# A transformer block and two hybrid attention and retention layers: V of the attention heads projected in one product of 512 columns, V stationary in the retention heads

## The reference

```python
def hybrid_layer(x, norm_gain, w_in, w_out, rel_bias, cos, sin):
    hn = rms_norm_2(x, norm_gain)
    proj = hn @ w_in                       # 1024 -> 4096
    aq, ak, av, ag, rq, rk, rv, rg = jnp.split(proj, cuts, axis=-1)    # 512 each
    ya = chunked_rel_attention(aq, ak, av, rel_bias)      # 8 heads of 64
    yr = chunkwise_retention(rq, rk, rv, cos, sin)        # 4 heads of 128, rms_norm_2 per head
    y = jnp.concatenate([ya * silu(ag), yr * silu(rg)], axis=-1)
    return x + y @ w_out
```

## Time and profile before

| | us |
|---|---|
| median of three runs | 1198.65 |
| the three runs | 1197.14, 1198.65, 1198.66 |
| the profiled execution | 1195.86 |
| span of its trace | 1193.6 |
| PE busy | 1179.8 |
| DVE busy | 870.6 |
| ACT busy | 592.5 |
| POOL busy | 260.1 |

### The profile page before, as it was taken

One profiled execution on the slowest core, in us unless ns is written; L12 is line 12 of the kernel. 1 busy time (PEld: TensorE's weight loads), 2 busy tenths in 40 slices (PEclk: granted clock), 3 DMA queues, 4 the chain that ended last, 5 costly groups with the idle time before them and its releaser, 6 DMA issues.

```text
span 1193.6 us, 15642 instructions
## 1 busy us (share of the span) xinstructions
PE 1179.8 (99%) x5813; PEld 999.4 (84%) x5813; DVE 870.6 (73%) x1417; ACT 592.5 (50%) x1067; POOL 260.1 (22%) x283
## 2 busy tenths in 40 slices
PE   9999999999999999999999999999999999999998
PEld 7887788888888888888888889899888889899886
DVE  6789855656786578546776788887867788988746
ACT  6777623234343344324435477755445577754542
POOL 0220499932000000000004511012323311012300
PEclk9999999999999999999999999999999999999999
DMA  6455433333422433243333366652213376663621
GB/s 191 143 169 170 142 101 94 88 106 89 139 77 68 140 106 89 72 124 104 90 102 92 104 189 183 194 161 72 84 58 109 98 209 199 173 175 116 158 71 71
DMA packets 218767, 146.84 MB, mean 123 GB/s; under 512 B 6250, under 2 KB 209476, under 8 KB 218564
## 3 DMA queue, kind: packets, MB, share of 16 engines
q1 hardware_dynamic: 218692, 145.86, 42.4%
HBM read 127.49 MB, written 18.35 MB: 122 GB/s over the span
## 4 chain that ended last, share of the span: by engine, by line
PE 86%; DVE 7%; ACT 5%; issue 2%; DMA 0%; DVEq 0%; POOL 0%; ACTq 0%; POOLq 0%
PE ps L191 85%; ACT a_p L161 1%; DVE tmp L164 1%; DVE a_p L178 1%; ACT whi L161 1%; ACT b_p L161 1%; ACT b_sets L161 1%; DVE wlo L164 1%; DVE a_pd L182 1%; DVE x1h L167 1%; PE ps L194 1%; DVE a_zc L167 0%; DVE tmp L167 0%; ACT x1h L161 0%; DVE b_pt L164 0%
## 5 line engine op out<-in xcount | busy, mean ns | idle before, releaser
L161 ACT ACTIVATE whi<-raw 128x1024 fp32r<-128x1024 f32 (+1 forms) x198 | 206.3, 1050 | 281.6 <-PE ps L191 270.3
L164 DVE TENSOR_TENSOR wlo<-raw,whi 128x1024 fp32r<-128x1024 f32 (+1 forms) x192 | 248.7, 1302 | 47.9 <-ACT whi L161 46.9
L191 PE MATMUL ps<-x0h,whi 128*128 128x512 f32 x1008 | 254.5, 391 | 1.8 <-ACT whi L161 1.8
L191 PE MATMUL ps<-x0h,wlo 128*128 128x512 f32 x1008 | 254.4, 391 | 0.0
L191 PE MATMUL ps<-x0l,whi 128*128 128x512 f32 x1008 | 254.2, 390 | 0.0
L191 PEld LDWEIGHTS ps<-x0l,whi 128*128 128x128 f32 x1008 | 188.2, 188 | 39.1 <-DVE x0l L167 0.5
L191 PEld LDWEIGHTS ps<-x0h,whi 128*128 128x128 f32 x1008 | 187.1, 188 | 39.8 <-ACT whi L161 2.0
L191 PEld LDWEIGHTS ps<-x0h,wlo 128*128 128x128 f32 x1008 | 187.7, 188 | 38.1
L164 POOL TENSOR_TENSOR sums<-sums,sq 128x512 f32<-128x512 f32 x28 | 43.3, 1559 | 416.7 <-ACT sq L161 416.7
L191 PE MATMUL ps<-x1h,wlo 128*128 128x512 f32 x304 | 82.3, 389 | 0.0
L191 PE MATMUL ps<-x1h,whi 128*128 128x512 f32 x304 | 82.3, 389 | 0.0
(11 more groups left out here) (188 smaller groups left out, 1659.1 us busy)
## 6 DMA issues: line engine op xcount, KB each, us to landing
raw<-in_w_in_dram SPq DMA_DIRECT2D x98, 512.0 KB, 4.3
raw<-in_w_up_dram SPq DMA_DIRECT2D x44, 512.0 KB, 3.8
raw<-in_w_out_dram SPq DMA_DIRECT2D x24, 512.0 KB, 3.9
turned<-b_pd SPq DMA_DIRECT2D x16, 640.0 KB, 3.2
raw<-in_w_down_dram SPq DMA_DIRECT2D x16, 512.0 KB, 4.0
b_px<-turned SPq DMA_DIRECT2D x32, 160.0 KB, 3.6
b_p<-turned SPq DMA_DIRECT2D x32, 160.0 KB, 3.5
turned_a<-a_pd SPq DMA_DIRECT2D x6, 512.0 KB, 2.6
```

The source lines that it names most:

```text
L161: return AC.put(lambda e: e.activation(o, i, func, **kw), after, AC, 1)
L164: return on.put(lambda e: e.tensor_tensor(o, a, b, op), after, on, 1)
L191: return PE.put(lambda e: e.matmul(o, l, r, start=start, stop=stop), after, PE if mark else None, 1)
```

## The change

Five parts:

1. V of the attention heads. The two `project_v(0)` and `project_v(1)` become one `project_va`: X0 stationary, 512 columns of weights moving, 96 matmuls in place of 192, in four PSUM banks at once (7, 5 and two of the projections' three). Their results leave the banks in the last quarter. The order of tiles is now k0 q0 k1 q1 V g0 k2 q2 g1 k3 q3 g2 g3 in place of k0 q0 V g0 k1 q1 g1 k2 q2 V g2 k3 q3 g3. Head 0 starts at step 13 in both layers, head 6 at 49 in place of 48.
2. Retention heads. V is stationary and the probabilities move: 4 x 2 matmuls with the high half and 4 with the low half, of 512, 384, 256 and 128 columns, all into bank 7, one step later. The result has features on partitions already, so the four transposes go. ACT copies it and squares it; DVE block-transposes and sums the squares; one matmul with `FOLD` (16 columns) ends the sum; DVE reads it, POOL (for the last head DVE) makes 1/sqrt, DVE spreads it and multiplies.
3. Buffers: the retention heads' order of p buffers is 0, 1, 2, 0, and a copy of `RB2` and `h_final` use PD in place of PX.
4. `unit_a` alternates between banks 6 and 7 (u is g here) in place of bank 7 alone.
5. The two small DMAs of the start are issued on ACT's queue.

```diff
-            order = [4, 0, "v", 12, 5, 1, 13, 6, 2, "v", 14, 7, 3, 15]
+            order = [4, 0, 5, 1, "va", 12, 6, 2, 13, 7, 3, 14, 15]
...
+                if m == "va":
+                    for k0 in range(0, 8, 2):
+                        plan_tm(wi2, k0, 1024, 2, 512)
...
-        t_mix = dma(rows[0][0:8, :], mix_norm[0].rearrange("(a b) -> a b", b=128), d_mix)
-        t_id = dma(CA[:, 0:128], const_a[:, 0:128], d_id)
+        t_mix = dma(rows[0][0:8, :], mix_norm[0].rearrange("(a b) -> a b", b=128), d_mix, on=AC)
+        t_id = dma(CA[:, 0:128], const_a[:, 0:128], d_id, on=AC)
...
-            o, free = PS[7], claim(7)
+            o, free = PS[6 + u], claim(6 + u)
...
-            bank_free[7] = [a1, a2]
+            bank_free[6 + u] = [a1, a2]
...
-        hps, pxs, rps = Slots(p_bufs, [0], p_free), Slots(p_bufs, [2, 1], p_free), Slots(p_bufs, [0, 1], p_free)
+        hps, pxs, rps = Slots(p_bufs, [0], p_free), Slots(p_bufs, [2, 1], p_free), Slots(p_bufs, [0, 1, 2, 0], p_free)
...
+            def project_va():
+
+                ws, bs = [W.take() for _ in range(4)], [7, 5, banks.next(), banks.next()]
...
+                for kb in range(4):
+                    i, wh, wl = ws[kb]
+                    for t, b in enumerate(bs):
+                        for part in range(3):
+                            for kk in range(2):
+                                k = 2 * kb + kk
+                                x, tx = (X0.lo, X0.tl) if part == 1 else (X0.hi, X0.th)
+                                w, tw = (wl, W.lo) if part == 2 else (wh, W.hi)
+                                first, end = k == 0 and part == 0, k == 7 and part == 2
+                                tok = mm(PS[b][:, :], x[:, k, 128 * t:128 * t + 128], w[:, kk, :], first, end,
+                                         after=[tx[k], tw[i], claim(b) if first else ()], mark=end or (kk, part, t) == (1, 2, 3))
+                                hook()
+                        if kb == 3:
+                            begin(evac(b, t, tok))
+                    W.done[i] = tok
+                    begin(W.split())
...
-                yield 1
-                ends, free = [], [claim(3), claim(4)]
-                for t in range(4):
-                    o = PS[3 + t // 2][:, 256 * (t % 2):256 * (t % 2) + 256]
-                    for kt in range(t + 1):
-                        c = PT_K[kt] + 128 * (t - kt)
-                        mm(o, hi[:, c:c + 128], v_at(s // 2, kt)[:, s % 2, :], kt == 0, False, after=[th, tl, tok_v[s // 2], free[t // 2]])
-                        tp = mm(o[:, 0:128], lo[:, c:c + 128], v_at(s // 2, kt)[:, s % 2, 0:128], False, kt == t, mark=kt == t)
-                    ends.append(tp)
+                yield 2
+                o, free = PS[7], claim(7)
+                vs = [v_at(s // 2, kt)[:, s % 2, :] for kt in range(4)]
+                for kt in range(4):
+                    c, a0 = 128 * kt, PT_K[kt]
+                    mm(o[:, c:512], vs[kt][:, 0:128], hi[:, a0:a0 + 512 - c], kt == 0, False, after=[th, tok_v[s // 2], free])
+                    mm(o[:, c:512], vs[kt][:, 128:256], hi[:, a0:a0 + 512 - c], False, False)
+                for kt in range(4):
+                    c, a0 = 128 * kt, PT_K[kt]
+                    tp = mm(o[:, c:512], vs[kt][:, 0:128], lo[:, a0:a0 + 512 - c], False, kt == 3, after=tl, mark=kt == 3)
...
+                t1 = act(out, o[:, :], after=[tp, th, tl])
+                t2 = act(sq, o[:, :], ACT.Square, after=[tp, th, tl])
+                bank_free[7] = [t1, t2]
+                yield 1
+                k, t, free = T.take()
+                t3 = blocks(t, sq, after=[t2, free])
+                t3 = add_up(part, t.rearrange("p (j b) -> p j b", b=32), after=[t3, tl])
+                T.free[k] = [t3]
+                yield 1
+                bank = 5 if i == 3 else 6
+                tp = mm(PS[bank][:, 0:16], FOLD[:, :], part, True, True, after=[t3, va["fold"], claim(bank)], mark=True)
+                yield 1
+                rr, t4, t_read = rsqrt_of(PS[bank][:, 0:16], 16, 1.0 / 128, 1e-6, tp, on=DV if i == 3 else PO, c=c, read=DV)
+                bank_free[bank] = [t_read]
+                if i < 3:
+                    yield 3
+                t5 = spread(sq, rr, t4)
+                t6 = tt(out, out, sq, ALU.mult, after=[t5, t1])
...
-                free = claim(7)
-                for t in range(4):
-                    tp = tr(PS[7][:, 128 * t:128 * t + 128], ob[t // 2][:, t % 2, :], IDENT, after=[t5[t], free], mark=t == 3)
-                rps.free[kp] = [tp]
...
-            at_step(13 - l, head(0, 1))
+            at_step(13, head(0, 1))
             for i in range(1, 8):
-                at_step(13 - l + 6 * i if i == 0 else 12 + 6 * i, head(i))
+                at_step(49 if i == 6 else 12 + 6 * i, head(i))
             evs = []
-            for s in range(4):
-                evs += [ev_k(s), ev_q(s)] + [s // 2] * (s % 2 == 0) + [ev_g(s)]
+            for s in range(2):
+                evs += [ev_k(s), ev_q(s)]
+            evs += [None, ev_g(0), ev_k(2), ev_q(2), ev_g(1), ev_k(3), ev_q(3), ev_g(2), ev_g(3)]
```

More of the change, by code:

```diff
@@ L1434, in ret @@
                 yield 1
-                part = lambda a: a.rearrange("p (t c) -> p t c", c=256)
-                both = [part(PS[3 + h][:, :]) for h in range(2)]
-                ob = [tiles(pb[:, 256 * h:256 * h + 256]) for h in range(2)]
-                tmp = [tiles(pb[:, 512 + 256 * h:768 + 256 * h]) for h in range(2)]
-                t1 = [act(tmp[h], both[h][:, :, 128:256], after=[ends[2 * h + 1], th, tl]) for h in range(2)]
+                out, sq, part, c = pb[:, 0:512], pb[:, 512:1024], pb[:, 1024:1040], pb[:, 1040:1088]
@@ L1441, in ret @@
+                t1 = act(out, o[:, :], after=[tp, th, tl])
+                t2 = act(sq, o[:, :], ACT.Square, after=[tp, th, tl])
+                bank_free[7] = [t1, t2]
                 yield 1
-                t2 = [tt(ob[h], both[h][:, :, 0:128], tmp[h], ALU.add, after=[t1[h], tl]) for h in range(2)]
-                bank_free[3], bank_free[4] = [t2[0]], [t2[1]]
+                k, t, free = T.take()
+                t3 = blocks(t, sq, after=[t2, free])
+                t3 = add_up(part, t.rearrange("p (j b) -> p j b", b=32), after=[t3, tl])
@@ L1462, in ret @@
                 k, t, free = T.take()
-                t3 = tt(t, PS[7][:, :], s2, ALU.mult, after=[tp, ts2, free])
-                bank_free[7] = [t3]
+                t3 = tt(t, out, s2, ALU.mult, after=[t6, ts2, free])
+                rps.free[kp] = [t3]
                 s2s.free[k3] = [t3]
```

45 lines of the change are left out of this document (26 added, 19 removed).

## The result

| us | before | after |
|---|---|---|
| median of 20 runs each | 1198.66 | 1195.66 |
| lowest and highest of them | 1196.01, 1200.28 | 1194.01, 1196.86 |
| the profiled execution | 1195.86 | 1196.49 |
| span of its trace | 1193.6 | 1194.7 |

The ratio is 0.9980 [0.9974, 0.9987]: 2.4 us faster by the ratio, 3.0 by the medians, where 10.7 were predicted. 1195.66 lies above the range. The two traces even show 1.1 us more. Both can be so: the profiled execution of before is faster than all of its 20 runs, and that of after is one of the slower ones. Of the 82 executions of before that were taken beside the experiments, the 8 with a mean granted clock of 0.999 took 1195.97 to 1196.29 us, the 56 with 0.995 or 0.996 took 1198.12 to 1200.69, and one of 1684.23 at 0.654 is left out of the ratios. The profiled execution of before (0.999) is of the first kind.

The account below looks back on a forecast made before the run. The kernel was taken as bound by PE's own instructions from start to start plus its few pauses. Terms of 2.5 + 5.1 + 0.9 + 2.2 = 10.7 us off 1197.9 gave 1187.2 us, range 1182.3 to 1193.3.

Parts of the forecast that it names:

- V of the attention heads, -2.5: Attention heads, both layers: 96 matmuls of 512 columns replace 192 of 256, saving 1.2 us per layer, 2.5 us in all.
- rival (b): A matmul's fixed part is as small as the skill page says, so V saves 0.5 us, giving 1189.2; chance 2%.
- The head pause: Pause of 0.58 us per layer at head 6 for q3's low half moves to head 4, same size; net 0.
- The retention product, -5.1: Retention heads: fewer stationary loads, no transposes, a FOLD matmul added; 0.64 us saved per head, 5.1 us over 8 heads.
- `b_pt` waits, -0.9: Retention head 2, both layers: PE's waits of 0.45 us for the probabilities' low half both go, 0.9 us saved.
- Rivals (a): New PE pauses for DVE (head 4 +2, X1[6] +1, FOLD 2.4) give back 5.4 us, so 1192.6; chance 12%.
- (c): Slower than before: PE waits at each FOLD matmul for DVE; with 3 us each 13 us longer, 1211; chance 3%.
- `unit_a`, -2.2: `unit_a`: alternating banks ends two waits, but the low half is then late; 1.1 us gained each, 2.2; bounds 0.9, 3.9.
- X1[6], 0: Retention head 2, layer 0, ends one step later; about 0.9 us slack left, possible wait 0 to 1 us, taken at 0.
- The prediction is wrong if k2 waits for a bank: Sign of failure: k2, the second product after V, needs back one of V's four banks; its wait was costed at nothing.
- The start, 0: Kernel start: SP issues x 0.86 us earlier, but x is not late, so 0 us gained, at most 0.2.
- The base: Starting time 1197.9 us, the middle between the inner two (1197.14, 1198.65) of the profiled execution and three runs.

Follow-up runs that it names:

- only_v: The kernel before with V of the attention heads as one 512-column product alone, with its tile order and head steps: 1196.50 us, ratio 0.9976.
- a_hfin: The changed kernel with layer 0's eight h_final begun at steps 99 to 106 in place of 90 to 104: 1192.48 us, ratio 0.9946 to before.
- best1: The changed kernel with small DMAs on SP again, last stage's banks ordered 0, 1, 6, 2, h_final at steps 99 to 106: 1189.10 us, ratio 0.9917 to before.
- only_ret: The kernel before with only the new retention heads (V stationary, no transposes) and their p buffers: 1207.09 us, ratio 1.0069.
- a_dve2: The changed kernel with the third retention head's 1/sqrt on DVE too, without POOL and the delay: 1196.75 us, ratio 0.9987 to before.
- a_banks: The changed kernel with the last stage taking its banks in the order 0, 1, 6, 2 in place of 0, 1, 2, 6: 1192.64 us, ratio 0.9955 to before.
- only_start: The kernel before with only the two small DMAs of the start moved to ACT's queue: 1200.40 us, ratio 1.0007.
- a_sp: The changed kernel with the two small DMAs of the start on SP's queue again: 1194.78 us, ratio 0.9970 to before.
- a_ones: The changed kernel with 14 products of ones at the very start in place of 9: 1194.58 us, ratio 0.9971 to before.
- after_again: The changed kernel run once more, unchanged: 1196.33 us, ratio 0.9983 to before.
- a_fill: The changed kernel with 14 starting products of ones in place of 9 and seven more before the first product: 1193.11 us, ratio 0.9956 to before.

## Why the prediction was wrong

The direction was right, the size was not: 10.7 us against 3.0. Step by step:

**V of the attention heads, -2.5: right.** 2.45 us by `only_v`. That the Trainium skill's fixed part would make it 0.5, rival (b), is refuted. The head pause moved from head 6 to head 4 with its size, as said, and the cost of 0 held.

**The retention product, -5.1, and its `b_pt` waits, -0.9: right.** 1.86 us in place of 2.25, no transposes, FOLD 0.13 us and no wait in front of it. Rivals (a) in its FOLD part and (c) fall. Where nothing large stood in the way, the terms of parts 1 and 2 came to 3.9 us of the predicted 4.2 (layer 0 of `a_hfin`, layer 1 with the last stage in `best1`). What is missing is a new pause of 0.25 us per layer in front of the last retention head's scores. It is in `only_ret` and not in `only_v`, so it comes with part 2.

**`unit_a`, -2.2: mis-sized, 1.1.** The step "the high-half matmul would go at 121.0" took the high half as ready. ACT writes it, and PE waited 0.80 us for it, then 1.02 for the low half, where the sum had no wait for ACT and one for DVE that ends at 122.4. So two waits stand one behind the other where the sum had one. The value is within its bounds.

**X1[6], 0: the step that failed by its choice of value.** The bounds were 0 to 1 us, the wait is 1.25 us idle and about 1.4 from start to start. The prediction took the row 883.5 against 886.26 less the head's delay of one step (1.8 us) as 0.9 us of slack, named DVE's standing behind POOL's chain, and put it at 0. The cause it named was the right one in part: DVE stands 1.30 us for POOL. What the prediction didn't count is what DVE then has to do without a pause, 7.2 us up to the low half, with two `h_final` in them. Taking `h_final` away ended the wait (`a_hfin`), and moving POOL's chain to DVE didn't (`a_dve2`).

**The last retention product one step later: the step that is missing.** The prediction counted this move for the head itself ("one step later") and for X1[7], but not for the work that the product had stood in front of. Before, its 2.25 us covered the evacuation of g7's bank. It now stands behind eight matmuls of the next stage, and PE reaches the bank too early: 2.4 us of pause and 1.4 for the product at the lower clock, with the matmuls around it 4.1 us by the last stage of `a_banks`. This is the largest part of the miss, and a term that the sum doesn't have at all. "The prediction is wrong if k2 waits for a bank" looked for the right kind of wait at the wrong product.

**The start, 0: the step that failed by its reading.** "x is not late" is right, but what PE takes up at 5.11 needs the identity as well, and the identity was moved behind x and onto a second queue, where it landed at 6.2 in place of 3.1. The prediction looked at what the moved DMAs free, not at what happens to them. By the two traces that is 4.2 us; by the runs of `only_start` and `a_sp` about 1 to 1.6, and by the means of the seven starts on each queue 1.3. The trace of before was the fastest of its seven, and other starts on SP's queue lose part of it to the lower clock too.

**The base.** The 1195.86 of the profiled execution stands below all 20 runs of before, 2.8 under their median. Its start took 17.43 us, the least of all traces, and it has no slow stretch behind `unit_a`. The prediction took the middle between it and the runs, 1197.9; from 1198.66 the forecast would have been 1188.0, 0.8 us nearer and still 7.7 us short.

The sum mended: 10.7 less 4.1 (bank), 1.4 (X1[6]), 1.1 (`unit_a`), 0.5 (the new pauses of 0.25 us) is 3.6 without the start. Less 1 to 1.6 for the start it is 2.0 to 2.6, where the runs show 2.4 by the ratio and 3.0 by the medians. With the 4.2 us of the two traces it is -0.6, where their spans show -1.1.

**What stays open.** By the runs `a_hfin` is worth 2.8 to 3.2 us, by its stretch 1.5. In both of its traces the pause in the last stage went without the slow stretch, which is worth the other 1.5; in those of after and of the five experiments with this pause and without that edit (`a_sp`, `a_dve2`, `a_ones`, `after_again`, `a_fill`) it went with it. With eight traces of eight and two comparisons of runs that fit, chance is the less likely account, but why an edit in layer 0 should do this isn't shown. The share of the start over all executions is known only to about 1 us. Of the 3 us of spread between executions that remain after a filled start, the slow stretch behind `unit_a` could make 1.6; no traces of such executions are at hand to tell.

## What to carry to other kernels

When a piece of PE's work moves later, price what it had covered: list the waits that stand directly behind its old place, bank reuse first, and count the matmuls from its new neighbours to each of them. When work is added to an engine that is nearly full in a stretch (here DVE, 17.2 of 19.2 us), compare the added time, standing for other engines included, with the slack of the last result due in that stretch, not with that of its own step. Leave a small transfer that others wait for ahead of the large ones; here a second queue didn't bring it past them. And before a sum starts from one profiled execution, see whether it is a typical one.

## What the runs showed of the hardware

A pause of PE of 1 to 2 us can be followed by a stretch at the lower clock level, and needn't be, in one and the same program. Behind the waits of 0.8 and 1.0 us in `unit_a`, eight matmuls took 3.3 us at 0.54 granted in `after_again` and 1.8 at 1.00 in after. Behind a wait of 2.12 us at that place they took 3.1 us in `only_start`, which differs from before in the queue of two DMAs alone, and 1.8 in before. At the bank of the last stage 2.26 us of waiting were followed by 3.2 us at 0.52 granted (after) and by none (`a_hfin`), and 5.11 us by 3.2 us at 0.50 (`only_ret`). In front of X1[6], waits of 1.25 us, and of 1.84 in two traces, were followed by none.

At the start, a pause of 1.86 us was followed by slow pairs until 12.7 in `after_again` and by none in `a_hfin` and `a_banks`, and one of 1.76 by none in before. In after the level wasn't up before the pause of 1.72 either: the transposes at 6.42 were slow already, up to 16.1. So the same program differs by 2.1 to 2.6 us in its start alone, and a pause that is taken away is worth more in some executions than in others.

Matmuls of 512 columns with their own stationary operand are 0.227 us apart and of 256 columns 0.120, at full clock: 13 ns beside the columns. The 64 KB of the identity landed 1.9 us after their issue as the second transfer of the kernel, and 4.8 us after it with 512 KB of x and 512 KB of weights issued ahead on another queue.
